# Modulation in four column groups: four blocks in the first stage, the others in the merge; h scaled in token chunks; no barrier between the opening and the heads

## The reference

```python
mod = (jnp.dot(jax.nn.silu(cond), w_ada) + b_ada).reshape(-1, 1, 6 * D)   # two rows: c_ctx and c
sh1, sc1, g1, sh2, sc2, g2 = jnp.split(mod, 6, axis=-1)
h = rmsnorm(x, norm1) * (1.0 + sc1) + sh1
x_in, bg, cg, q, zf, zb, iv, og, ga, gb = split_proj(jnp.dot(h, w_in))
...   # conv branch A, two-way HGRN2 branch B (8 heads)
mix = jnp.dot(jax.nn.sigmoid(ga) * ya + jax.nn.sigmoid(gb) * yb, w_o)
x = x + g1 * mix
h2 = rmsnorm(x, norm2) * (1.0 + sc2) + sh2
x = x + g2 * expert_choice_ffn(h2, w_router, w_e_gate, w_e_up, w_e_down)
```

## Time and profile before

| | before |
|---|---|
| median of 3 runs | 2588.87 us (2588.83 to 2588.98) |
| the profiled execution | 2586.46 us |
| its span | 2584.7 us |
| mean granted TensorE clock | 0.971 |
| PE busy | 2426.2 us (94%) |
| DVE, ACT, POOL busy | 1025.5 us (40%), 841.2 us (33%), 366.6 us (14%) |
| DMA, mean | 145 GB/s |
| products of the heads (L717), first start | 112.56 us |
| first matmul of the merge (L1409) | 1298.09 us |
| first matmul of the routing stage (L1643) | 1508.71 us |

### The profile page before, as it was taken

One profiled execution on the slowest core, in us unless ns is written; L12 is line 12 of the kernel. 1 busy time (PEld: TensorE's weight loads), 2 busy tenths in 40 slices (PEclk: granted clock), 3 DMA queues, 4 the chain that ended last, 5 costly groups with the idle time before them and its releaser, 6 DMA issues. The chain is left out here.

```text
span 2584.7 us, 47081 instructions
## 1 busy us (share of the span) xinstructions
PE 2426.2 (94%) x17645; PEld 2294.1 (89%) x17645; DVE 1025.5 (40%) x2630; ACT 841.2 (33%) x1989; POOL 366.6 (14%) x611
## 2 busy tenths in 40 slices
PE   7799999999999999999799989669999999999992
PEld 2499999999999999999799978369999999999992
DVE  2455453645455453645433344732222122222222
ACT  2454544454454544454322022111111111111112
POOL 0011110211111110211101124110101010101011
PEclk9899999999999999999999999879999999999996
DMA  7412112121212112121354234738877887788754
GB/s 277 171 44 63 51 52 64 37 78 30 77 44 62 51 52 64 37 79 30 98 205 151 73 118 141 274 98 291 280 242 255 290 276 244 257 291 280 237 190 163
DMA packets 368200, 375.95 MB, mean 145 GB/s; under 512 B 11803, under 2 KB 340539, under 8 KB 368096
## 3 DMA queue, kind: packets, MB, share of 16 engines
q1 hardware_dynamic: 353928, 326.58, 37.8%
q0 software_dynamic: 14160, 47.81, 6.5%
q10 hardware_dynamic: 10, 0.02, 0.0%
HBM read 330.82 MB, written 43.55 MB: 145 GB/s over the span
## 5 line engine op out<-in xcount | busy, mean ns | idle before, releaser
L717 PE MATMUL bank<-HT,W 128*128 128x384 f32 x5760 | 1047.9, 338 | 9.9 <-DVE bank L1214 9.9
L717 PEld LDWEIGHTS bank<-HT,W 128*128 128x128 f32 x5760 | 995.4, 188 | 13.3 <-DVE bank L1214 10.2
L2016 PE MATMUL bank<-XET,WEA 128*128 128x144 f32 x4096 | 511.2, 287 | 0.6 <-DVE XET L2088 0.6
L2016 PEld LDWEIGHTS bank<-XET,WEA 128*128 128x128 f32 x4096 | 505.9, 191 | 1.2 <-issue 0.7
L2031 PE MATMUL bank<-HID,WED 128*128 128x144 f32 x2048 | 257.8, 287 | 0.0
L2031 PEld LDWEIGHTS bank<-HID,WED 128*128 128x128 f32 x2048 | 252.6, 190 | 0.7
L1409 PE MATMUL bank<-YO,W 128*128 128x384 f32 x960 | 172.7, 337 | 19.2 <-ACT YO L1425 19.2
L1409 PEld LDWEIGHTS bank<-YO,W 128*128 128x128 f32 x960 | 169.0, 190 | 19.5 <-issue 19.5
L2047 ACT ACTIVATE SG<-bank 128x144 f32<-128x144 f32 x128 | 37.3, 291 | 409.5 <-PE bank L2016 409.5
L2117 DVE TENSOR_TENSOR GU<-SG,bank 128x144 f32<-128x144 f32 x128 | 39.0, 304 | 300.4 <-ACT SG L2051 300.4
L2055 ACT ACTIVATE YT<-bank 128x144 f32<-128x144 f32 x128 | 37.3, 291 | 274.3 <-PE bank L2031 274.3
(11 more groups left out here) (218 smaller groups left out, 2795.9 us busy)
## 6 DMA issues: line engine op xcount, KB each, us to landing
WEA<-in_w_e_gate_dram SPq DMA_DIRECT2D x64, 1024.0 KB, 5.1
WEA<-in_w_e_up_dram SPq DMA_DIRECT2D x64, 1024.0 KB, 10.5
WED<-in_w_e_down_dram SPq DMA_DIRECT2D x64, 1024.0 KB, 9.9
W_FULL<-in_w_in_dram SPq DMA_DIRECT2D x80, 512.0 KB, 3.7
AW<-in_w_ada_dram SPq DMA_DIRECT2D x10, 2048.0 KB, 9.1
sg_d<-QR SPq DMA_DIRECT2D x48, 192.0 KB, 1.9
GL<-sg_d POOLq DMA_DIRECT2D x48, 192.0 KB, 2.7
ya_d<-CY SPq DMA_DIRECT2D x24, 192.0 KB, 1.9
```

The costliest lines, as they stand in the source:

```text
L717: ins = nc.tensor.matmul(bank[:, 0:CH], W[:, slot, a, k, :], HT[:, b, k, at * CH:(at + 1) * CH], start=(i == 0 and k == 0), stop=(i == 2 a ...
L2016: ins = nc.tensor.matmul(PS[2 * s + f % 2][:, 0:NX], WEA[:, 4 * s + f // 2, k, (f % 2) * P:(f % 2 + 1) * P], XET[:, k, :], start=(k == 0), ...
```

## The change

In the opening only blocks 0 to 3 are computed. AW has four buffers, and SP issues their loads without waiting for PE. A block's 512 columns are cut into four parts of 128; part j goes to PSUM partitions 32j and 32j+1, so the matmuls of a block use four groups of weight columns. b_ada and norm1 are loaded in the same layout (BIX, NIX); DVE adds and scales all at once, PE transposes four 128 x 128 tiles, DVE copies the columns. The nine tiles of x are normalised, transposed and copied to SBUF without the modulation; then ACT and DVE scale and shift h in place in three chunks of 384 tokens, four k each, and split each chunk and one weight slot in turn. The opening's lists stand at the head of the heads' lists in one block; the clearing and the barrier between them are gone. Step kind f of head 0 waits for its chunk's parts.

The other eight blocks of 512 columns become sixteen of 256 in the merge, one behind step 0 of each weight block, loaded into one buffer AM in the place of weight slot 4, with the bias and norm2 in the layout of the groups (BI, NI); ACT stores the four vectors to mod_d. The merge's loops over s are unrolled. AWG, MG and their matmuls and adds leave the routing stage, and the store of MG leaves the experts.

```diff
+        AW = pro("AW", [P, 4, KT, 512])
...
+        def opening_sync(sp):
...
+            sp.dma_start(AW[:, 0], w_ada_v[:, :, 0:512]).then_inc(ada_in[0], 16)
+            sp.wait_ge(rows_zero, 2)
+            for j in range(4):
+                sp.dma_start(BIX[32 * j:32 * j + 2], ...).then_inc(rows_in, 16)
+                sp.dma_start(NIX[32 * j:32 * j + 2], ...).then_inc(rows_in, 16)
+            for b in range(1, 4):
+                sp.dma_start(AW[:, b], w_ada_v[:, :, b * 512:(b + 1) * 512]).then_inc(ada_in[b], 16)
+            for slot, off in enumerate((ZF, ZB, IV)):
+                wload(sp, slot, w_in_v, off)
...
+        def opening_act(act):
...
+            for t in range(TN + 1):
...
+                if t > 0:
+                    src, dst = normal_rows(t - 1, 1)
+                    act.wait_ge(xt_t, 2 * t)
+                    nc.scalar.activation(dst, src, ACT.Copy).then_inc(xt_act, 1)
...
+            high(0)
+            act.wait_ge(mod_ct, 1)
+            for n in range(NCH):
+                cols = slice(n * CH, (n + 1) * CH)
+                for k in range(4, KT):
+                    for lo_, hi_, c in chunk_parts(n):
+                        h = HT_FULL[:, 1, k, lo_:hi_]
+                        ins = nc.scalar.activation(h, h, ACT.Identity, bias=SH1T[:, k, c:c + 1],
+                                                   scale=A1T[:, k, c:c + 1])
+                ins.then_inc(full_act, 1)
+                act.wait_ge(full_dve, n + 1)
+                nc.scalar.activation(HT[:, 0, 0:4, cols], HT_FULL[:, 1, 0:4, cols], ACT.Copy).then_inc(h_hi, 1)
+                act.wait_ge(full_act, n + 1)
+                nc.scalar.activation(HT[:, 0, 4:KT, cols], HT_FULL[:, 1, 4:KT, cols], ACT.Copy).then_inc(h_hi, 1)
+                if n < 2:
+                    high(1 + n)
+
+        def opening_tensor(pe):
+            def ada(b):
+                pe.wait_ge(ada_in[b], 16)
                 for k in range(KT):
+                    for j in range(4):
+                        ins = nc.tensor.matmul(PS[1][32 * j:32 * j + 2, b * P:(b + 1) * P], CT[:, k, :],
+                                               AW[:, b, k, j * P:(j + 1) * P], start=(k == 0), stop=(k == KT - 1))
+                ins.then_inc(ada_mm, 1)
...
+            for b, n in enumerate((2, 3, 3, 1)):
+                ada(b)
+                for i in range(n):
+                    rows(t)
+                    t += 1
+            pe.wait_ge(mod_fix, 2)
+            for b in range(4):
+                ins = nc.tensor.transpose(PS[3][:, b * P:(b + 1) * P], MODX[:, b, :], IDENT)
+            ins.then_inc(mod_t, 1)
...
+        def opening_vector(dve):
...
+            for n in range(NCH):
+                cols = slice(n * CH, (n + 1) * CH)
+                for k in range(4):
+                    for lo_, hi_, c in chunk_parts(n):
+                        h = HT_FULL[:, 1, k, lo_:hi_]
+                        ins = nc.vector.tensor_scalar(h, h, A1T[:, k, c:c + 1], SH1T[:, k, c:c + 1],
+                                                      ALU.mult, ALU.add)
+                ins.then_inc(full_dve, 1)
+                if n == 0:
+                    low(0)
+                for half in range(2):
+                    ks = slice(4 * half, 4 * half + 4)
+                    dve.wait_ge(h_hi, 2 * n + half + 1)
+                    nc.vector.tensor_tensor(HT[:, 1, ks, cols], HT_FULL[:, 1, ks, cols],
+                                            HT[:, 0, ks, cols].bitcast(F32), ALU.subtract).then_inc(h_lo, 1)
+                if n < 2:
+                    low(1 + n)
...
+                    first = g == 0 and kind == "f"
+                    if first:
+                        pe.wait_ge(h_hi, 2 * at + 2)
...
+                opening_act(act)
                 act.sem_inc(gate_read, 6)
-                act.wait_ge(x_zero, 4)
...
+        AM = nc.alloc_sbuf_tensor_at("AM", [P, KT, GW], F32, offset=W_OFF + 4 * SLOT)
+        def mod_weights(eng, b):
+            eng.dma_start(AM[:], w_ada_v[:, :, 2 * D + b * GW:2 * D + (b + 1) * GW]).then_inc(am_in, 16)
...
+                    if p == 0:
+                        mod_weights(sp, 0)
...
                 for b in range(4, NB):
                     sp.wait_ge(m_product, (b - 3) * NCH)
                     wload(sp, b % 4, w_oa_v if b < KT else w_ob_v, (b % KT) * P)
+                    sp.wait_ge(am_mm, b - 3)
+                    mod_weights(sp, b - 3)
                     if b == KT + 3:
                         for slot in range(4):
                             sp.dma_start(WED[:, slot], w_o_v[:, :, slot * GW:(slot + 1) * GW]).then_inc(wo_in, 16)
+                for b in range(NB - 3, NB):
+                    sp.wait_ge(am_mm, b)
+                    mod_weights(sp, b)
...
+                def mod_rows(b):
+                    pe.wait_ge(am_in, 16 * b + 16)
+                    if b >= 2:
+                        pe.wait_ge(am_row, b - 1)
+                    for k in range(KT):
+                        for j in range(4):
+                            ins = nc.tensor.matmul(PS[4 + b % 2][32 * j:32 * j + 2, 0:64], CT[:, k, :],
+                                                   AM[:, k, 64 * j:64 * j + 64],
+                                                   start=(k == 0), stop=(k == KT - 1))
+                    ins.then_inc(am_mm, 1)
...
                                 ins.then_inc(m_product, 1)
+                                if n == 0:
+                                    mod_rows(p * KT + 4 * s + m)
...
+                    dve.wait_ge(am_mm, b + 1)
+                    nc.vector.tensor_tensor(BI[0:98, b], PS[4 + b % 2][0:98, 0:64], BI[0:98, b],
+                                            ALU.add).then_inc(am_row, 1)
...
-                dve.wait_ge(bg2_in, 16)
-                for i in range(2):
-                    dve.wait_ge(g2_mm, i + 1)
-                    cols = slice(i * 512, (i + 1) * 512)
-                    nc.vector.tensor_tensor(MG[:, cols], MG[:, cols], PS[1 + i][0:2, :],
-                                            ALU.add).then_inc(g2_row, 1)
...
-                sp.dma_start(mod_d[:, 3, :], MG[:]).then_inc(g2_out, 16)
-                sp.wait_ge(g2_out, 16)
```

More of the change, by code:

```diff
@@ L209, in wload @@
             eng.dma_start(W_FULL[:, slot, 1], src[:, :, ds(col, P)]).then_inc(weights_in[slot], 16)
[L211 to L239, removed]
@@ new lines, in opening_vector, with low @@
+            nc.vector.scalar_tensor_tensor(MODX[:, 2:4], MODX[:, 2:4], 1.0, NIX[:],
+                                           ALU.add, ALU.mult).then_inc(mod_fix, 1)
+            dve.wait_ge(mod_t, 1)
+            for dst, lo_ in ((SH1T, 0), (A1T, 256)):
+                ins = nc.vector.tensor_copy(dst[:], PS[3][:, lo_:lo_ + 256].rearrange("p (k r) -> p k r", r=32)[:, :, 0:2])
+            ins.then_inc(mod_ct, 1)
+            def low(slot):
+                dve.wait_ge(w_hi, slot + 1)
+                nc.vector.tensor_tensor(W[:, slot, 1], W_FULL[:, slot, 1],
+                                        W[:, slot, 0].bitcast(F32), ALU.subtract).then_inc(w_lo, 1)
@@ new lines, in opening_vector @@
+            dve.wait_ge(mod_ct, 1)
+            for n in range(NCH):
[8 more added lines that the diff above has]
+                    low(0)
+                for half in range(2):
+                    ks = slice(4 * half, 4 * half + 4)
[4 more added lines that the diff above has]
+                    low(1 + n)
@@ L448, in trunk, with opening_gpsimd @@
+            dve.wait_ge(xt_act, TN)
+            for i in range(2):
+                nc.vector.memset(PS[6 + i][:, 0:2 * P], 0.0)
+        def opening_gpsimd(pool):
+            for t in range(2):
+                pool.dma_start(XT[:, t], x_rows[t]).then_inc(x_in_s[t], 16)
+            for t in range(2, TN):
+                pool.wait_ge(xn_done, t - 1)
+                pool.dma_start(XT[:, t % 2], x_rows[t]).then_inc(x_in_s[t % 2], 16)
+            pool.wait_ge(mod_ct, 1)
         br = Region(nc, after_h, hi)
@@ L665, in after @@
                             sp.wait_ge(product, g * NS + j + 1)
-                            if last:
+                            if last and slot < 4:
                                 wload(sp, slot, w_oa_v, slot * P)
+                            elif last:
+                                pass
                             else:
@@ L1211, in filler @@
                         conv_dve(g, j)
-                for i in range(2):
-                    nc.vector.memset(PS[6 + i][:, 0:2 * P], 0.0).then_inc(x_zero, 1)
+                opening_vector(dve)
                 dve.sem_inc(ob_made, 1)
-                dve.wait_ge(x_zero, 4)
+                dve.wait_ge(x_zero, 2)
                 with dve.Fori(0, NH) as g:
@@ L1475, in _ @@
                     chunk(i)
-                with dve.Fori(0, 2) as s:
+                for s in range(2):
                     for m in range(4):
@@ L1688, in _ @@
                 pe.wait_ge(x1_g, 2 * TN)
-                for i in range(2):
```

(5 more changed lines are left out.)

393 lines of the change are left out of this document (183 added, 210 removed).

## The result

The changed kernel takes 2618.99 us (median of four, 2617.46 to 2623.09) against 2588.85 (2586.32 to 2588.98) for the kernel before, run beside it: a ratio of 1.0123 with a 95% interval of 1.0111 to 1.0134, so slower by 30 us. The prediction said 2615. The page's line of busy times shows TensorE at 91% of the span, where it was 94%.

What follows compares the result with a forecast made beforehand. It took TensorE, busy 94% of the span, as the bound, plus stretches with nothing ready. 2586.5 - 41 (opening) - 1.3 (tail) + 69 (merge) = 2613.2; with the profiled execution 2.4 below the median, 2615; range 2604 to 2628, 8 in 10: 2585 to 2642.

Steps and rivals of the forecast that it cites:

- Opening, modulation columns at 49.6: Opening: the chain of x sets the pace and the modulation columns stand at 49.6 us, bounds 44 and 54.
- Chunk phase of 21.8 us, held by gate_read: Opening: ACT's last rounding ends 21.8 us after the columns; gate_read's increment behind it starts head 0 at 71.5, gaining 41.
- No later wait of head 0: Head 0: no later wait replaces the opening's; DVE's subtraction of chunk 2 is ready before step 2 needs it.
- Own price of a block, 1.1 us in four groups: Merge: a block's 64 matmuls of 64 columns, four column groups side by side, take 1.1 us.
- rival of groups in series: Merge: block matmuls run one group after another, costing 16 x 2.3 us more, time 2652; chance 0.08.
- Landing 6.8 us behind the issue, waits of 2.9: Merge: AM's load lands 6.8 us after issue, behind the weight load; TensorE arrives at 4.0 and waits 2.9.
- The clock, 12 us: Merge: a lowered TensorE clock costs 1.0 us behind each of twelve waits, 12 in all.
- second rival: Merge: the clock falls at every wait, 12 x 3.1 us in place of 12, time 2640; chance 0.12.
- BI, NI and the adds at nothing: Merge: BI, NI, DVE's sixteen adds and ACT's stores lie beside steps of 4.16 us and cost nothing.
- The start of the merge: Stretch from the heads' last product to the merge's first: predicted difference 0.
- Tail, 1.3 us: Routing stage's tail: two blocks, MG and their adds go; gain 1.3 us from DVE's adds.
- loads in time: Merge: AM lands within 4.0 us, waits and clock loss vanish, merge costs 22, time 2568; chance 0.10, in time or nearly.

Runs made afterwards that it cites:

- second run: Changed kernel with ACT's increment of gate_read by six ahead of the opening's list instead of behind it; 2613.95 us, ratio 1.0096.
- eighth run: Changed kernel with gate_read released ahead of the opening, AM loaded ahead of the weight load, BI/NI loads after block 1's AM load, blocks behind step 1; 2553.64 us.
- fourth run: Changed kernel without the merge's sixteen modulation blocks and their loads, so the stored rows are the bias alone; 2538.76 us, ratio 0.9809.
- seventh run: On the first run, all 64 matmuls of a merge block in column group 0, DVE's add not reading the block; 2603.94 us, ratio 1.0066.
- first run: Changed kernel with AM's load issued once the previous block is multiplied, ahead of the weight-slot wait and weight load; 2563.60 us, ratio 0.9905.
- fifth run: Changed kernel with AM's load still issued after the previous weight block's last step, but ahead of the weight load on the queue; 2577.99 us, ratio 0.9963.
- ninth run: On the fourth run, an unread 512 KB load into the fifth weight slot put back ahead of the last ob_d store; 2541.41 us, ratio 0.9825.
- sixth run: Changed kernel with only four of each merge block's 64 matmuls, all loads, waits, adds and stores kept; 2606.07 us, ratio 1.0076.

## Why the prediction was right

The forecast, its sign and its mechanism held, with some sizes off, and errors that offset one another helped the number. (The prediction's own sum gives 2613.2 + 2.4 = 2615.6; it says 2615.) By its steps:

- **Opening, modulation columns at 49.6**: 51.7. The last tile landed 2.4 us later than worked out.
- **Chunk phase of 21.8 us, held by gate_read**: ACT's last rounding ended 73.05 - 51.70 = 21.4 us behind the columns, as predicted. But the increment did not wait for the two roundings that stand before it in the list: the product started at 70.26, just as ACT's queue had started the first of them. So the release came 18.6 us behind the columns in place of 21.9, which is 3.3 early, while the columns were 2.1 late: 71.5 became 70.3, and 41 us became 42.3 at the first product and 42.8 at the heads' end. That these lie so close is luck. That chunk 0's data did not set the start is shown by the second run.
- **No later wait of head 0**: right.
- **Own price of a block, 1.1 us in four groups**: 1.07 busy, and 1.26 with the restart of the products (eighth run less fourth). The rival of groups in series is refuted by the seventh run.
- **Landing 6.8 us behind the issue, waits of 2.9**: the median landing is 6.8 us, the waits of blocks 1 to 12 have a mean of 3.5, from 1.2 to 5.4. The waits come to 43.8 us where the prediction had 57 - 16 x 1.1 = 39.4. The cause (the place on the queue and the late issue) is shown by the first and fifth runs. The loads of blocks 5 to 7 landed 7.9, 9.0 and 7.6 us behind their issue, and their waits of 4.23, 5.30 and 3.97 are 4.8 us above three of 2.9, about what the sum was short of; no run here shows what held these three.
- **The clock, 12 us**: 281.7 (changed) - 223.25 (eighth run) - 43.8 (waits) = 14.7; TensorE's busy time for the same 2176 instructions says the same, 236.71 against 222.11. Of thirteen waits eight brought the clock down, for some 1.8 us each. The prediction had twelve at 1.0, so that 12 came near 14.7 is in part luck. The second rival, a fall at every wait, is out: five waits of 1.20 to 3.16 us left the clock up, and nine of 0.74 to 1.18 in the fifth run. The section "HAM oscillation — how this bites in real kernels" of the Trainium skill's page "TensorE: Matmul & The Clock Gate" tells of a kernel whose DMA waits all outlast what the gate tolerates, and whose clock falls at each. The six longest waits here, 3.28 to 5.44 us, agree with it, and waits that the gate tolerates are no case of it; the prediction took it for a rule on every wait. Which of the waits between 2 and 3.3 us bring the clock down stays open.
- **BI, NI and the adds at nothing**: right; DVE stood 8.87 us for NI, but TensorE's three steps of that time ran without a gap.
- **The start of the merge**: missed. The sum put this stretch at nothing: the load into the fifth weight slot, whose place AM took, no longer stands ahead of the heads' last store, and the prediction doesn't price that. It gave 3.1 us (ninth run) and offset a third of what the merge's sum had too low.
- **Tail, 1.3 us**: 1.2.

The merge's products: 69 predicted, 77.9 measured, less the 3.1 at its start. The terms that were too small are the waits (43.8 for 39.4), the clock (14.7 for 12) and the blocks (20.1 for 17.6). The 0.9 us in the experts' stretch was not tested. Of TensorE's first 10 us of expert products the clock is 0.72 after and 0.76 before, which would be some 0.4 of it.

The nearest wrong turn would have been the rival "loads in time". It needed a landing in 4.0 us, which no load of AM had (5.0 ahead of the weight load, fifth run; the shortest of any run 4.8), or an earlier issue, which takes two lines in another place: in the first run it comes two steps earlier, and the time is 2563.6 against the 2568 that the prediction gave that case.

## What to carry to other kernels

Work moved into a dense stage costs its own time (here 20 us) plus the waits for its loads that nothing covers (44) and what these take from the clock (15): count from the semaphore that lets the load go, with all that stands ahead of it on the queue, to the instruction that wants it, and compare that with the work between. If a single buffer is refilled, issue the refill when the buffer comes free, not when the neighbour's load is due; that order was worth 55 us here. A barrier that is removed can live on as the order of one engine's list, and a transfer ahead of a stage's last store is part of that stage's end.

## What the runs showed of the hardware

- How long a wait is did not alone decide whether TensorE's clock fell from 2.4 to 1.2 GHz. In the changed kernel it stayed up over waits of 2.24, 2.54, 2.91 and 3.16 us and fell over 2.66 and 2.84 and over all six from 3.28 to 5.44; in the sixth run it fell over 2.17 and 2.21 and stayed up over 2.64 and 2.83. In the fifth run it stayed up over all nine from 0.74 to 1.18.
- 64 matmuls of 64 columns with two columns of weights took 3.73 us in one column group and 1.07 in four.
- A semaphore increment that stands by itself in ACT's list released TensorE at 70.26, when of the two activations just ahead of it one had begun (70.19) and the other had not (71.58); they ended at 73.05. Here such an increment did not tell that the work ahead of it was done.
- A 512 KB load issued 0.47 us ahead of a stage's last store held the next stage's first load back by 2.4 us (5.65 against 3.28) and its first product by 3.3 (19.5 against 16.2).
